# Scores of both query tiles issued in one place, the doubling multiply ahead of the tile sum, and the last four weight blocks gone through once for each token half

## The reference, cut to what matters

```
# block 1: for each of 8 head pairs
o = hgrn2_scan(q, k, v, log_g)                       # gated linear scan, here as 7 levels of pair products
s = q @ k.T * 64**-0.5 + rel_bias                    # band attention; p = softmax(s) @ v
# block 2: for each of 8 head pairs
s = q @ k.T * 64**-0.5 + rpb ; p = softmax(s) @ v    # neighbourhood attention
x = x + merged @ w_out
x = x + (silu(gate) * val) @ w_down                  # conv FFN, 5504 wide
return x * rsqrt(mean(x * x, -1) + 1e-6) * norm_final
```

## Time and profile before

| | |
|---|---|
| median of 3 runs | 2795.0 us |
| profiled execution, its own time | 2795.07 us |
| its span, first to last instruction | 2793.3 us |
| TensorE (PE) busy | 2774.0 us, 99% |
| VectorE (DVE) busy | 2075.8 us, 74% |
| ScalarE (ACT) busy | 1473.8 us, 53% |
| HBM read | 517.22 MB, 186 GB/s over the span |
| granted TensorE clock | 0.998 |

### The profile page before, as it was taken

How to read it: one execution, slowest core, us unless ns; L and a number is a source line. 1 busy time by engine, 2 the same in 40 slices (tenths; PEclk the granted TensorE clock), 3 DMA queues, 4 the chain that set the end, 5 groups by cost and what they waited for, 6 DMA issues and landing times.

```text
span 2793.3 us, 40592 instructions
## 1 busy us (share of the span) xinstructions
PE 2774.0 (99%) x15440; PEld 2376.8 (85%) x15440; DVE 2075.8 (74%) x3193; ACT 1473.8 (53%) x2182; POOL 63.6 (2%) x72
## 2 busy tenths in 40 slices
PE   9999999999999999999999999999999999999998
PEld 6888888888888888888888888888888888888886
DVE  5687888887677777777786677678778777777775
ACT  5556555565444444444465555556555555555554
POOL 0000000000000000000050000000000000000000
PEclk9999999999999999999999999999999999999999
DMA  7554555555555555555555555555555555555553
GB/s 267 187 177 158 187 171 170 169 187 186 179 196 193 191 188 186 192 193 185 213 198 183 195 178 178 186 174 186 185 200 190 187 189 190 191 191 189 190 195 129
DMA packets 157010, 521.98 MB, mean 187 GB/s; under 512 B 28944, under 2 KB 31376, under 8 KB 156560
## 3 DMA queue, kind: packets, MB, share of 16 engines
q1 hardware_dynamic: 155808, 517.31, 54.4%
q10 hardware_dynamic: 1008, 2.08, 0.2%
HBM read 517.22 MB, written 2.10 MB: 186 GB/s over the span
## 4 chain that ended last, share of the span: by engine, by line
PE 93%; DVE 5%; issue 1%; ACT 0%; DMA 0%; SPq 0%; ACTq 0%; DVEq 0%
PE acc L424 35%; PE acc L429 17%; PE psX L424 5%; PE psT L424 5%; PE acc_first L424 5%; PE psT L429 3%; PE psX L429 3%; PE acc_first L429 2%; DVE w_lo L1204 1%; PE acc L463 1%; PE acc L461 1%; PE acc L462 1%; DVE HS L1286 1%; DVE AT L1303 1%; PE psT L708 1%
## 5 line engine op out<-in xcount | busy, mean ns | idle before, releaser
L1204 DVE TENSOR_TENSOR w_lo<-w_raw,w_hi 128x1024 fp32r<-128x1024 f32 x958 | 1171.5, 1228 | 351.6 <-ACT w_hi L783 321.5
L783 ACT ACTIVATE w_hi<-w_raw 128x1024 fp32r<-128x1024 f32 x958 | 1003.6, 1055 | 532.2 <-PE acc L424 265.8
L424 PE MATMUL acc<-XU,w_hi 128*128 128x512 f32 x2848 | 930.8, 398 | 0.0
L429 PEld LDWEIGHTS acc<-XU,w_lo 128*128 128x128 f32 x2848 | 535.3, 188 | 122.4
L424 PE MATMUL acc<-XY,w_hi 128*128 128x512 f32 x1792 | 579.0, 397 | 0.0
L429 PE MATMUL acc<-XU,w_lo 128*128 128x256 f32 x2848 | 560.1, 278 | 0.0
L424 PEld LDWEIGHTS acc<-XU,w_hi 128*128 128x128 f32 x2848 | 447.7, 189 | 4.1 <-issue 2.7
L429 PEld LDWEIGHTS acc<-XY,w_lo 128*128 128x128 f32 x1792 | 336.7, 188 | 77.9
L429 PE MATMUL acc<-XY,w_lo 128*128 128x256 f32 x1792 | 352.6, 278 | 0.0
L424 PEld LDWEIGHTS acc<-XY,w_hi 128*128 128x128 f32 x1792 | 278.7, 189 | 8.2 <-issue 5.3
L788 ACT ACTIVATE cross<-acc 128x256 f32<-128x256 f32 x242 | 92.6, 383 | 355.9 <-PE acc L424 355.9
(11 more groups left out here) (346 smaller groups left out, 3281.9 us busy)
## 6 DMA issues: line engine op xcount, KB each, us to landing
w_raw<-in_weights SPq DMA_DIRECT2D x962, 512.0 KB, 3.3
bias<-in_rel_bias SPq DMA_DIRECT2D x8, 384.0 KB, 3.9
bias<-in_rpb_back SPq DMA_DIRECT2D x32, 96.0 KB, 6.0
hT<-in_x_t SPq DMA_DIRECT2D x8, 256.0 KB, 8.5
G<-in_norm_rows SPq DMA_DIRECT2D x2, 1024.0 KB, 7.5
out_dram<-G SPq DMA_DIRECT2D x2, 512.0 KB, 4.0
G<-in_pair_masks ACTq DMA_DIRECT2D x1, 960.0 KB, 5.5
out_dram<-G ACTq DMA_DIRECT2D x2, 384.0 KB, 4.6
```

The source lines that it names most:

```text
L424: return nc.tensor.matmul(bank[:, :], hi[:, k, col:col + P], X[:, k0 + k, :], start=first and k == 0, stop=last and k == nk - 1 and k % 2 ...
L429: return nc.tensor.matmul(bank[:, 0:T], lo[:, k, col:col + P], X[:, k0 + k, 0:T], start=False, stop=last and k == nk - 1 and k % 2 == 0, s ...
L783: act.activation(w_hi[s][:, 0:n], w_raw[s][:, 0:n], ACT.Copy).then_inc(hi_done, 1)
L1204: V.tensor_tensor(w_lo[s][:, 0:n], w_raw[s][:, 0:n], w_hi[s][:, 0:n].bitcast(F32), ALU.subtract).then_inc(lo_ready, 1)
```

## The change: what it does

1. **heads1, TensorE.** `scores` now does both query tiles as one job, after block 12, into separate columns (tile 0 in 0:128, tile 1 in 128:384 of each bank), without the wait on `scores_read`. `tile_pairs` moves from after block 12 to after block 13. `level_products(6)` stays after block 11, alone.
2. **heads1, DVE.** In step b = 6+n the order is now `low_part`, `take_pairs(n)`, the doubling multiply, `widen_spans(n+1)` with its gather, and then the tile sum; `widen_spans(0)` comes in step 5. Both fronts are in step 12, both backs in step 14.
3. **heads1, ACT.** All exponentials at b = 13.
4. **heads2.** Both score tiles after block 6 (columns 0:256 and 256:512), both fronts at b = 7, exponentials at b = 8, backs at b = 9.
5. **ffn2last.** Blocks 12 to 15 are gone through twice: first all products of token half 0, which then signal `first_half`, then all of half 1. Residual add, weighing, squares, root, scaling and output are done for each half by itself; each half goes out in three DMAs (768, 768 and 512 columns), six in all. The last columns are scaled in place in `final_last`.

```
@@ tensor
-            def scores(a, nk, x):
+            def scores(x):
                 def job(i):
-                    if a == 0:
-                        pe.wait_ge(S(f"qk_ready{x}"), i + 1)
-                        pe.wait_ge(S(f"yb_ready{x}"), i)
-                    else:
-                        pe.wait_ge(S(f"scores_read{x}"), i * 2 + 1)
-                    for h, bank in enumerate((psS, psX)):
...
+                    pe.wait_ge(S(f"qk_ready{x}"), i + 1)
+                    pe.wait_ge(S(f"yb_ready{x}"), i)
+                    for a in range(NT):
+                        for h, bank in enumerate((psS, psX)):
+                            q0, at = 64 * h, score_columns(a, x)
+                            done = nc.tensor.matmul(bank[:, at], wk(6)[q0:q0 + 64, a * P:(a + 1) * P],
+                                                    wk(7)[q0:q0 + 64, 0:at.stop - at.start], start=True, stop=True)
                     done.then_inc(S(f"scores_full{x}"), 1)
...
-                11: [scores(0, P, 1), level_products(6)],
-                12: [tile_pairs],
-                13: [scores(1, T, 1)],
+                11: [level_products(6)],
+                12: [scores(1)],
+                13: [tile_pairs],
...
-                6: [scores(0, T, 2)],
-                8: [scores(1, T, 2)],
+                6: [scores(2)],
...
+            last = [(b, s) for b, s in enumerate(FFN["ffn2last"]) if on_last_chunk("ffn2last", s)]
+            for b, s in last:
+                done = token_downs(last_phase, 0, b, s, XY, (0,), 0)
+            done.then_inc(S("first_half"), 1)
+            for b, s in last:
+                token_downs(last_phase, 0, b, s, XY, (1,), 1)
@@ vector, heads1
-                    if 0 <= n < LEVELS:
-                        widen_spans(n, i)
                     if b != 14:
                         low_part(p, i, b)
                     if 0 <= n < LEVELS:
                         take_pairs(n, i)
+                    if 0 <= n < LEVELS - 1:
+                        next_spans(n)
+                    if 0 <= n + 1 < LEVELS:
+                        widen_spans(n + 1, i)
...
                     if b == 14:
+                        softmax_back(0, P, 1, i)
                         softmax_back(1, T, 1, i)
                         low_part(p, i, b)
-                    if b == 11:
+                    if b == 12:
                         softmax_front(0, P, 1, i)
-                    if b == 13:
                         softmax_front(1, T, 1, i)
@@ vector, heads2
                     if b == 7:
                         softmax_front(0, T, 2, i)
-                    if b == 9:
                         softmax_front(1, T, 2, i)
...
-                    if b == 8:
+                    if b == 9:
                         softmax_back(0, T, 2, i)
-                    if b == 10:
                         softmax_back(1, T, 2, i)
@@ vector, the end
-            for a in range(NT):
-                weigh(a, D // CHUNK - 1, final_last[:, a * CHUNK:(a + 1) * CHUNK])
-            dve.wait_ge(S("sqf_added"), NT * (D // CHUNK))
...
+                if a:
+                    dve.wait_ge(w_used, last_phase.block(0, last_phase.blocks - 1) + 1)
+                else:
+                    dve.wait_ge(S("first_half"), 1)
+                chunk_out(last_phase, 0, FF2 // KB - 1, LAST_CHUNK, (a,))
+                weigh(a, LAST_CHUNK, final_last[:, a * CHUNK:(a + 1) * CHUNK])
+                dve.wait_ge(S("sqf_added"), NT * LAST_CHUNK + a + 1)
+                mark(V.tensor_reduce(tok_r1[:, a:a + 1], square_sums[:, 4 * a:4 * a + 4], AX_X, ALU.add), S("out_sum"), a + 1)
+                dve.wait_ge(S("out_rstd"), a + 1)
+                for part in (Gf[:, a * D:a * D + OUT_ACT], final_last[:, a * CHUNK:(a + 1) * CHUNK]):
+                    V.tensor_scalar(part, part, small[:, 6 + a:7 + a], None, ALU.mult).then_inc(S("out_scaled0"), 1)
@@ scalar
-                    if b == 11:
+                    if b == 13:
                         softmax_exp(0, P, 1, i)
-                    if b == 13:
                         softmax_exp(1, T, 1, i)
...
-                    if b == 7:
+                    if b == 8:
                         softmax_exp(0, T, 2, i)
-                    if b == 9:
                         softmax_exp(1, T, 2, i)
```

More of the change, by code:

```diff
@@ L297, in token_part, with on_last_chunk @@
             return Gf[:, a * D + c * CHUNK:a * D + (c + 1) * CHUNK]
+        def on_last_chunk(name, step):
+            return name == "ffn2last" and down_units(step)[0][0] == LAST_CHUNK
         def complete(step):
@@ L400, in _ @@
                                 load_x(q)
[L401 to L407, removed]
+            for a in range(NT):
+                for c, (c0, c1) in enumerate(((0, OUT_ACT), (D - CHUNK, D))):
+                    sp.wait_ge(S("out_scaled0"), 2 * a + c + 1)
+                    part = final_last[:, a * CHUNK:(a + 1) * CHUNK] if c else Gf[:, a * D + c0:a * D + c1]
+                    sp.dma_start(out[0, a * P:(a + 1) * P, c0:c1], part).then_inc(S("out_done"), 16)
+            sp.wait_ge(S("out_done"), 16 * 6)
         @block.tensor
@@ L684, in ffn @@
                     if name.startswith("ffn2"):
-                        token_downs(p, i, b, s, A)
+                        if not on_last_chunk(name, s):
+                            token_downs(p, i, b, s, A, range(NT), 1)
                     else:
@@ L710, in token_downs @@
                         done = nc.tensor.matmul(bank[:, :], x_lo, hi[:, e, :], start=False, stop=k == nk - 1, skip_group_check=True)
-                done.then_inc(w_used, 1)
+                if used:
+                    done.then_inc(w_used, used)
+                return done
             ffn("ffn1first", 0, XY, XU, S("act1_ready"), operand=one_by_one(x_ready, 0), sums=KD)
@@ L1084, in _, with final_squares @@
             rstd(rs[:, :], psS[:, 0:T], D, eps_rms, rs1[:, :], rs_ready)
-            def final_squares(c):
+            def final_squares(c, halves):
                 g = chunk_number("ffn2last", 0, FF2 // KB - 1, c)
-                for a in range(NT):
+                for a in halves:
                     act.wait_ge(S("chunk_out"), NT * g + a + 1)
@@ L1135, in _ @@
             ffn2("ffn2last", 0, late)
[L1136 to L1148, removed]
+            act.wait_ge(S("out_copied"), NT * LAST_CHUNK)
+            for a in range(NT):
+                final_squares(LAST_CHUNK, (a,))
+                act.wait_ge(S("out_sum"), a + 1)
+                link(act.activation(small[:, 4 + a:5 + a], tok_r1[:, a:a + 1], ACT.Ln, bias=eps_rms, scale=1.0 / D))
+                act.activation(small[:, 6 + a:7 + a], small[:, 4 + a:5 + a], ACT.Exp, scale=-0.5).then_inc(S("out_rstd"), 1)
+                act.wait_ge(S("out_rstd"), a + 1)
+                part = Gf[:, a * D + OUT_ACT:(a + 1) * D - CHUNK]
+                act.activation(part, part, ACT.Copy, scale=small[:, 6 + a:7 + a]).then_inc(S("out_scaled1"), 1)
+                act.wait_ge(S("out_scaled1"), a + 1)
+                act.dma_start(out[0, a * P:(a + 1) * P, OUT_ACT:D - CHUNK], part).then_inc(S("out_done"), 16)
         @block.gpsimd
@@ L1624, in ffn2 @@
                         for chunk, k, nk in down_units(s):
-                            if k == nk - 1:
-                                chunk_out(p, i, b, s.group, chunk)
+                            if k == nk - 1 and not on_last_chunk(name, s):
+                                dve.wait_ge(w_used, p.block(i, b) + 1)
+                                chunk_out(p, i, s.group, chunk, range(NT))
                         if name == "ffn2last" and b and b % 4 == 0:
@@ L1631, in ffn2, with chunk_out @@
                 return late
-            def chunk_out(p, i, b, group, c):
-                dve.wait_ge(w_used, p.block(i, b) + 1)
+            def chunk_out(p, i, group, c, halves):
                 g = chunk_number(p.name, i, group, c)
-                for a in range(NT):
+                for a in halves:
                     bank, h = down_banks[g % 2][a][:, :], token_part(a, c)
```

34 lines of the change are left out of this document (13 added, 21 removed).

## The result

The changed kernel takes 2780.9 us (median of 4 runs, 2779.76 to 2781.22) against 2795.17 us of before (4 runs): ratio 0.9948, 95% interval 0.9936 to 0.9959. It is 14.3 us faster. The direction and the three sources were right, and one term was sized at less than half.

The account below looks back on a forecast made before the run. TensorE, busy 99% of the span, was taken as the bound. Gains of 5.4 (heads1), 1.4 (heads2) and 4.2 us (the end) made 11.0 off 2795.07, forecasting 2784.0 us, with a range of 2782.0 to 2789.5.

Parts of the forecast that it names:

- the three sources: Gains forecast in heads1 (5.4 us), in heads2 (1.4 us) and at the end (4.2 us).
- Part 1: Scores in one place in heads1: 0.55 us a head, 0.38 of `tile_pairs` wait and 0.17 of entry and exit.
- part 3: heads2, both score jobs in one place: 0.18 us a head saved, 1.4 us in all.
- The bodies are kept at full price, since the same matmuls run: Score jobs in heads1: both bodies still cost 0.42 and 0.63 us when put in one place.
- one entry into and one exit from the half-array form: Going into and out of matmuls reading 64 of 128 partitions, once less per head: 0.17 us in heads1.
- Part 2: DVE's order in heads1: level 5's wait goes (0.22 a head), level 6 gains 0.1, level 4 just in time.
- the probabilities in heads2: DVE's last probabilities in heads2 taken as in time by a few tenths; bound 0.3 late, 2.4 us lost.
- Part 4: The end, done by token halves: span ends 7.7 us behind the add instead of 11.9, 4.2 saved.
- the prediction's estimate by the page: Output writes at the end, by the skill's 2.0 us fixed and 436 GB/s: the whole ends 0.3 us later.
- the first three: Key chain behind, 2788.8 (chance 0.15); only the end shortened, 2790.9 (0.10); probabilities late, 2803.5 at 1.3 us late (0.05).
- The fourth: Scores in heads1 drain between the tiles, 2.7 us lost: 2786.7, within the range and part of the forecast's chance.
- The lower edge of the range: Whole kernel: 6.2 in heads1, 1.4, and 4.5 at the end give 2783.0; one more us for unpriced waits.

Follow-up runs that it names:

- Experiment 7: Changed kernel with `tile_pairs` back behind block 12, ahead of the scores, with DVE's new order or its old one: 2780.98 and 2781.5 us.
- experiment 1: Changed kernel with the scores in two places again in heads1 and heads2, DVE's order staying new: 2785.88 us.
- experiment 6: Changed kernel with DVE's old order in heads1, widening and doubling multiply behind the tile sum, TensorE's places staying new: 2781.53 us.

## Why the prediction was off, step by step

- **Part 1, the wait of `tile_pairs`: right in size, but not for the reason given.** It went, worth 0.40 a head (forecast 0.38). I gave it to the step of the widening and the later place of the job. Experiment 7 shows that both could have been left out: the front's move out of step 11 was enough, by the rows there.
- **Part 1 and part 3, the step that failed: "The bodies are kept at full price, since the same matmuls run".** The same matmuls run, but 0.2 us of each old body belonged to the change of form and not to its passes. The term "one entry into and one exit from the half-array form" was sized at 0.17 in heads1 and 0.18 in heads2, and measures 0.39 and 0.43 (experiment 1, and the repeats of the heads). That is 8 x (0.22 + 0.25) = 3.8 us, of which 16 x 0.19 = 3.0 are the two jobs themselves (1.18 for 1.37, 1.39 for 1.58); in heads1 the rest is that undelayed jobs take 0.37 and not 0.39, in heads2 it isn't taken apart further. It is the whole difference between the 14.7 us of the three sums and the forecast's 11.0; the medians, 14.3 apart, lie 0.4 below that, less than the first products' start varies. The bodies in the earlier trace rows, 0.42 for 128 columns and 0.63 for 256, already showed it: had they been columns alone, the second would have been twice the first.
- **Part 2: right.** Level 5's wait went (0.24), level 6 got one of 0.13 (forecast 0.1), level 4 was in time. The value of the order by itself is about 1 us (0.11 a head, 1.0 in the traces of experiment 6), too little for the times to show.
- **Part 3, the probabilities in heads2: right.** No wait of TensorE on them appeared. In the first head they were done at 1568.13 (1567.78 + 0.35), 0.27 ahead of the start of block 11's last product (1568.40), where the kernel before had 0.03.
- **Part 4, the end: right.** 4.2 us, both forecast and in the changed kernel, 4.1 alone. The end lay 7.8 behind the add, between the 7.7 of the rows and the 8.0 that the prediction's estimate by the page gives. The Trainium skill (DMA: Bandwidth & Descriptors, Two cost components) states that fit for DMAs issued by GpSimd, and these writes go out on SP and ACT; no sum rested on it.
- **The rivals.** None of the first three came about. The fourth, a drain between the tiles, was the reverse of what I should have asked: how much of the old bodies was drain. The lower edge of the range took the price of the bodies as certain, and so had only 1 us for everything not priced; the measured time needed 2.1.

## What to carry to other kernels

A short job in another form of matmul costs its passes plus a fixed part, and that part shows only in small part as idle time. (The idle time of the weight loads ahead of the scores, about 0.25 us a place, went from 7.9 us in 32 places to 4.0 in 16.) Read the fixed part from jobs of two lengths: what doesn't scale with the columns is the price of the place. Before work is moved into one place for this reason, price the round trip and not only the gap ahead of it. And where one engine's chain feeds another just in time, take work that nobody waits for out of that chain before changing the order of the rest.

## What the runs showed of the hardware

The round trip from the full to the half-array form and back cost 0.39 us in heads1 and 0.43 in heads2 where a second place was given up or put back, 0.41 by the sum over one job, and 0.37 to 0.40 where a full-form matmul was put between the tiles. The same float32 job in the full form had no overhead that the rows could tell (2.18 us reckoned, 2.20 measured). A level job whose gather ended 0.19, 0.20 and 0.31 us behind the start of the last product ahead of it was delayed by 0.11, 0.13 and 0.24 us. The first 32 products, which follow the first loads, varied in their last start between 21.0 and 22.2 us over the traces, that is by more than a small edit is worth; counting from there removed it.
